# A hybrid decoder trunk on one core: delta-rule steps without GpSimd, z tiles between the k and v tiles, and a transpose in place of half of the inverse products

## Chip, cores, metric

The kernel runs on one core of a Trainium2 chip. The metric is the device time of one execution in microseconds (us), as the median of several runs. Engine names in the profile: PE is TensorE, DVE is VectorE, ACT is ScalarE, POOL is GpSimd, SP is SyncE, which issues the weight loads.

## What is computed

Two layers, each a half-step SwiGLU FFN, a token mixer and a second half-step FFN, on 336 tokens (256 prompt, 64 decode tokens of 8 sequences, 16 meta tokens), width 1024, FFN width 2816, all in float32. The mixer's input projection gives q, k, v, z (512 columns each), two gates, and b, c, h of a short convolution group. The reference, cut to what the change touches:

```python
qkv = silu(causal_dw_conv(qkv_ext, conv_gdn))
q = l2_normalize(q) * DK ** -0.5;  k = l2_normalize(k)
G = cumsum(g); diff = G[..., :, None] - G[..., None, :]
d_strict = exp(where(strict, diff, -inf)); d_incl = exp(where(incl, diff, -inf))
tmat = beta[..., None] * (k @ k.T) * d_strict + eye
u = triangular_solve(tmat, beta * v)              # and w, from k
qk = (q @ k.T) * d_incl
nv = u - w @ s;  o = (q * exp(G)) @ s + qk @ nv;  s = e_last * s + k_tail.T @ nv
o = rms_norm(o) * silu(z);  out = concat([o, gate_b * conv(gate_c * h_in)]) @ w_out
```

## The kernel before

**Products.** Each float32 product is made of three one-pass products in fp32r: a weight chunk lands in `RAW`, ACT copies its high part to `WH` (L694), DVE subtracts to get the low part `WL` (L939), and PE multiplies XH by WH, XL by WH and XH by WL (L1310 to L1312, the helper `three`). There are three chunk slots. ACT and DVE split chunk c+2 (`split_ahead`) while PE works on chunk c. Chunks are split in two halves, "hi" on ACT and "lo" on DVE.

**FFN.** 22 up chunks (gate and up tile of 128 features each), then 8 output tiles. `entry` interleaves the first two chunks as the input's tiles arrive. DVE's `up_tile(c)` scales both tiles (GR, UR: L1021, L1022), splits chunk c+2 unless c is 0, then does HF and HL (L1027, L1029). So chunk 3 is split in `up_tile(1)`.

**Mixer.** `mixer_steps` writes one list of steps that all engines walk, each doing its own share. The 28 tiles of the projection come in the order of `PROJ`: 12 of qkv (q, k, v), 4 z, 4 b, then c and h in pairs. From tile 4 on a tile is cut into three parts (`("part", i, p)`: 3, 3 and 2 of its 8 k steps), and the stretch behind each part is a slot, numbered from 0. Other work is put in slots by hand (`slot_work`): the gates (`gate_cols`, `gate_g`, `cum`, `gb`), the convolution of a qkv tile (`tap` on ACT, three taps on DVE in `conv` L1053, `silu` on ACT), the sums of squares (`sq` on ACT, `sq_rows` on PE L1496), `norms`, the scores `qk` and `kk` of each of the three token blocks t (order 2, 0, 1). A planner (`fill`) puts the delta-rule steps of `delta_stages` in the free room, at most two with PE products a slot, with LAG 2 slots between a step and what needs it.

**The triangular inverse**, per block t: `pair` (POOL, L654) masks DA into MI, `unit` (DVE, L1185) subtracts it from the identity, `nt` is its transpose (PE L1461, copied to NI by ACT L862). Then for each level m = 2, 4, ... (six levels for blocks 0 and 1, three for block 2): `x` is DA times NI, masked into XB (DVE L1191); `y` and `yt`, planned as one step, are the correction of NI and that of its transpose MI, four 128x128 products each (PE L1463), subtracted by DVE (L1196, L1200). POOL also masks QKM (L660) beside `x` of level 2.

**PSUM.** Products of four heads (L1463) and transposes (L1461) rotate over banks 5 to 7: a group waits until the one three before it has been read (`bank_free`); the third (`gb` of block 2) waits for the reading of tile 4 too, which had bank 7. A waiting instruction holds back all behind it on its engine.

## Time and profile before

| | us |
|---|---|
| median of 3 runs | 1552.85 |
| lowest, highest | 1552.75, 1554.69 |
| profiled execution: device time | 1553.45 |
| its span, first to last instruction | 1551.7 |
| PE busy | 1474.9 |
| DVE busy | 882.7 |
| ACT busy | 608.3 |
| POOL busy | 58.5 |

The span is one execution; engines overlap, so the busy times are not to be added. PE's granted clock is given per stretch: 1.00 is 2.4 GHz, 0.50 is 1.2 GHz, and a value between them is a stretch that has both. The two layers show nearly the same pattern 768 us apart; times below are of layer 0.

### The profile page before, as it was taken

Reading aid. Unit: us, or ns where it says so; the run is one execution under the profiler, and the core shown is the slowest. Engines: PE = TensorE matmul, PEld = TensorE weight load, DVE = VectorE, ACT = ScalarE, POOL = GpSimd, SP = SyncE. Lnnn points to the kernel's source line nnn. Section 1 sums busy time; section 2 is a strip of 40 time slices with the busy share of each in tenths; the row PEclk is TensorE's granted clock in tenths of the full one; section 3 lists DMA queues with packets and bytes.
Section 4 is the critical chain, followed back from the end, with each engine's and each line's share of the span. In section 5 each row is a group of like instructions: output and inputs, shape, how many; then the busy total and the mean of one; then the engine's idle time right before and its main releaser. Section 6 shows DMA issues by size and latency. Waiting matters only on the chain.

```text
span 1551.7 us, 22995 instructions
## 1 busy us (share of the span) xinstructions
PE 1474.9 (95%) x9696; PEld 1431.4 (92%) x9696; DVE 882.7 (57%) x1471; ACT 608.3 (39%) x953; POOL 58.5 (4%) x144
## 2 busy tenths in 40 slices
PE   6999999998999999999989999999899999999996
PEld 6999999878988999999989999998799889999996
DVE  4655534786458665554375554357854676656433
ACT  4533434552213543433354433345422235443431
POOL 0000001012000000000000000010210000000001
PEclk9999999999999999999999999999999999999998
DMA  7444344221113344434454443432211143444342
GB/s 262 136 136 147 123 146 156 69 94 59 37 46 129 124 137 150 148 119 149 144 187 136 137 147 128 148 121 91 88 45 56 55 144 121 138 149 155 130 150 90
DMA packets 48613, 191.11 MB, mean 123 GB/s; under 512 B 6048, under 2 KB 7328, under 8 KB 48000
## 3 DMA queue, kind: packets, MB, share of 16 engines
q1 hardware_dynamic: 47520, 183.22, 35.9%
q0 software_dynamic: 992, 6.44, 1.0%
q8 instruction: 77, 1.26, 0.3%
q14 instruction: 24, 0.20, 0.0%
HBM read 183.20 MB, written 6.43 MB: 122 GB/s over the span
## 4 chain that ended last, share of the span: by engine, by line
PE 84%; DVE 9%; ACT 4%; issue 2%; DMA 1%; SPq 1%; POOL 0%; DVEq 0%; ACTq 0%; POOLq 0%
PE PS L1310 23%; PE PS L1312 22%; PE PS L1311 22%; PE PS L1463 6%; DVE CV L1053 2%; DVE WL L939 2%; PE PS L1350 2%; PE PS L1355 2%; PE PS L1351 2%; PE PS L1618 1%; PE PS L1570 1%; DMA RAW<-in_w_up 1%; ACT WH L694 1%; PE PS L1461 1%; DVE X L997 1%
## 5 line engine op out<-in xcount | busy, mean ns | idle before, releaser
L1310 PE MATMUL PS<-XH,WH 128*128 128x336 f32 (+1 forms) x1728 | 558.3, 323 | 7.6 <-DVE WL L939 6.6
L1312 PE MATMUL PS<-XH,WL 128*128 128x336 f32 (+1 forms) x1728 | 547.1, 317 | 0.0
L1311 PE MATMUL PS<-XL,WH 128*128 128x336 f32 (+1 forms) x1728 | 546.5, 316 | 0.0
L939 DVE TENSOR_TENSOR WL<-RAW,WH 128x1024 fp32r<-128x1024 f32 (+1 forms) x312 | 399.3, 1303 | 198.3 <-ACT WH L694 198.2
L694 ACT ACTIVATE WH<-RAW 128x1024 fp32r<-128x1024 f32 (+1 forms) x312 | 345.8, 1120 | 214.7 <-DMA RAW<-in_w_down 172.5
L1310 PEld LDWEIGHTS PS<-XH,WH 128*128 128x128 f32 x1728 | 327.7, 190 | 28.2 <-issue 25.0
L1311 PEld LDWEIGHTS PS<-XL,WH 128*128 128x128 f32 x1728 | 328.2, 190 | 0.0
L1312 PEld LDWEIGHTS PS<-XH,WL 128*128 128x128 f32 x1728 | 327.8, 190 | 0.0
L1310 PE MATMUL PS<-HH,WH 128*128 128x336 f32 (+1 forms) x704 | 221.0, 314 | 0.0
L1312 PE MATMUL PS<-HH,WL 128*128 128x336 f32 (+1 forms) x704 | 220.4, 313 | 0.0
L1311 PE MATMUL PS<-HL,WH 128*128 128x336 f32 (+1 forms) x704 | 220.2, 313 | 0.0
L1021 DVE TENSOR_TENSOR GR<-PS,RB 128x336 f32<-128x336 f32 (+1 forms) x88 | 44.3, 503 | 194.8 <-PE PS L1312 194.7
L1311 PEld LDWEIGHTS PS<-HL,WH 128*128 128x128 f32 x704 | 132.4, 188 | 0.0
L1312 PEld LDWEIGHTS PS<-HH,WL 128*128 128x128 f32 x704 | 132.2, 188 | 0.0
L1310 PEld LDWEIGHTS PS<-HH,WH 128*128 128x128 f32 x704 | 132.1, 188 | 0.0
L762 ACT ACTIVATE HH<-HF 128x336 fp32r<-128x336 f32 (+1 forms) x88 | 42.4, 482 | 208.4 <-DVE HF L1027 208.4
L760 ACT ACTIVATE SG<-GR 128x336 f32<-128x336 f32 (+1 forms) x88 | 42.2, 480 | 118.1 <-DVE GR L1021 118.1
L1350 PE MATMUL PS<-XH,WH 128*128 128x336 f32 (+1 forms) x192 | 65.3, 343 | 23.3 <-DVE WL L939 12.6
L1029 DVE TENSOR_TENSOR HL<-HF,HH 128x336 fp32r<-128x336 f32 (+1 forms) x88 | 44.4, 505 | 48.2 <-ACT HH L762 48.2
L1351 PE MATMUL PS<-XH,WL 128*128 128x336 f32 (+1 forms) x192 | 64.4, 339 | 0.0
L1350 PEld LDWEIGHTS PS<-XH,WH 128*128 128x128 f32 x192 | 40.2, 209 | 24.8 <-DVE WL L939 12.5
L1053 DVE SCALAR_TENSOR_TENSOR CV<-EXT,PAR_ALL,CV 128x360 f32<-128x360 f32 x72 | 42.5, 592 | 17.7 <-ACT CV L789 16.0
(223 smaller groups left out, 1370.8 us busy)
## 6 DMA issues: line engine op xcount, KB each, us to landing
RAW<-in_w_up SPq DMA_DIRECT2D x176, 512.0 KB, 4.7
RAW<-in_w_down SPq DMA_DIRECT2D x64, 704.0 KB, 4.1
RAW<-in_w_in SPq DMA_DIRECT2D x56, 512.0 KB, 4.5
RAW<-in_w_out SPq DMA_DIRECT2D x16, 512.0 KB, 4.3
SEQ_S<-in_states SPq DMA_DIRECT2D x2, 2048.0 KB, 10.6
out_state_s<-SEQ_S POOLq DMA_DIRECT2D x2, 2048.0 KB, 8.4
X<-in_x SPq DMA_DIRECT2D x8, 168.0 KB, 6.1
out_y<-X POOLq DMA_DIRECT2D x8, 160.0 KB, 2.1
```

The source lines that it names most:

```text
L694: act.activation(WH[slot][:, cols], RAW[slot][:, cols], ACT.Copy).then_inc(split_hi.sem, 1)
L762: act.activation(hidden(HH, c, n), HF[k][:, 0:n], ACT.Copy).then_inc(h_hi.sem, 1)
L939: dve.tensor_tensor(WL[slot][:, cols], RAW[slot][:, cols], WH[slot][:, cols].bitcast(F32), ALU.subtract).then_inc(split_lo.sem, 1)
L1021: dve.tensor_tensor(GR[k][:, 0:n], PS[:, up_bank(c, 0), 0:n], RB[:, 0:n], ALU.mult).then_inc(gate_scaled.sem, 1)
L1029: dve.tensor_tensor(hidden(HL, c, n), HF[k][:, 0:n], hidden(HH, c, n).bitcast(F32), ALU.subtract).then_inc(h_lo.sem, 1)
L1053: ins = dve.scalar_tensor_tensor(cv, src[:, n, tap:tap + length - taps + 1], PAR_ALL[:, layer, col:col + 1], cv, ALU.mult, ALU.add)
L1310: pe.matmul(out, wh, xh, start=first, stop=False)
L1311: pe.matmul(out, wh, xl, start=False, stop=False)
L1312: return pe.matmul(out, wl, xh, start=False, stop=last)
L1350: pe.matmul(out, wh, XH[:, kt, 0:n], start=(kt == 0), stop=False)
L1351: pe.matmul(out, wl, XH[:, kt, 0:n], start=False, stop=False)
L1463: ins = pe.matmul(out[:, h, :], lhsT(h), rhs(h), start=True, stop=True)
```

## The change

1. **GpSimd leaves the delta steps.** `pair` goes; its product is done on DVE inside `unit`, which now follows `kk` of its block directly. QKM's mask goes: `gb` takes the minimum with a table (0 where kept, -1e4 elsewhere) instead of with 0, so the exponential is zero there.
2. **`mirror`.** `yt` stays only at the last level. At the others MI is made by four transposes of NI on PE, and ACT copies them. `y` is a step of its own; `x` of the next level waits for `y`, `y` of the next level for `mirror`.
3. **Tile order.** `TILES` puts z tiles between k and v tiles. v's convolutions move to slots 22 to 37, `silu` of z goes right behind its tile. `cum`, `gb` and the convolutions of the first tiles go a slot later, and evacuations of tiles 2 and 3 behind `gate_cols`.
4. **Table load.** ACT loads the table of Exp at the start of the mixer, ahead of the first taps.
5. **FFN.** Chunk 3 is split in `up_tile(0)`, on ACT ahead of that tile's Silu.
6. **Buffers.** XM0 and XM1 lie over SQX and ACCY; EXT's v tiles lie beyond NI and MI, so the units need wait only for POOL's copies of q and k (`qk_hist`).

```diff
-NO_PRODUCTS = ("pair", "unit", "o_inv", "o_low", "spread")
+NO_PRODUCTS = ("unit", "o_inv", "o_low", "spread", "mirror")
+TILES = [("qkv", n) for n in range(6)] + [("z", 0), ("qkv", 6), ("qkv", 7), ("z", 1), ("qkv", 8), ("z", 2), ("qkv", 9), ("z", 3),
...
-        after["pair", t] = []
-        after["unit", t] = [(("pair", t), LAG)]
+        after["unit", t] = []
         for m in levels:
-            after["x", t, m] = [(("nt", t) if m == 2 else ("yt", t, m // 2), LAG)]
-            after["yt", t, m] = [(("x", t, m), LAG)]
+            after["x", t, m] = [(("nt", t) if m == 2 else ("y", t, m // 2), LAG)]
+            if m < levels[-1]:
+                after["y", t, m] = [(("x", t, m), LAG)]
+                after["mirror", t, m] = [(("y", t, m), LAG)]
...
-    slot_work[2] += [("cum",), ("lo", 1, 1)]
-    slot_work[3] += [("gb", ORDER[0]), ("gb", ORDER[1])]
+    slot_work[2] += [("lo", 1, 1)]
+    slot_work[3] += [("cum",)]
+    slot_work[4] += [("gb", ORDER[0])]
+    slot_work[5] += [("gb", ORDER[1]), ("gb", ORDER[2])]
...
+    earliest.update({("unit", t): scores_at + 2 * n + 2 for n, t in enumerate(ORDER)})
...
                 for c in range(N_UP):
-                    if c > 0:
+                    if c == 0:
+                        split_ahead(layer, AT_UP[s] + 1)
+                    elif c > 1:
                         split_ahead(layer, AT_UP[s] + c)
                     up_tile(c, c % 2)
...
             def mixer(layer):
+                act.preload_act_table(ACT.Exp)
...
+                    elif what == "mirror":
+                        evacuated(act.activation(MI[:, step[1], :, :], group(step, layer), ACT.Copy))
...
-                    if c > 0:
-                        split_ahead(layer, AT_UP[s] + c)
+                    if c != 1:
+                        split_ahead(layer, AT_UP[s] + max(c, 1))
...
-                            ins = dve.tensor_scalar(DA[:, t, h, :], gb[:, h, :], GC[:, t, h:h + 1], 0.0, ALU.subtract, ALU.min)
+                            ins = dve.scalar_tensor_tensor(DA[:, t, h, :], gb[:, h, :], GC[:, t, h:h + 1], barred(t),
+                                                           ALU.subtract, ALU.min)
...
-                        dve.wait_ge(pair_part.sem, pair_part.at(NTH["pair", t], layer))
+                        own(("kk", t), layer)
+                        ch.step(dve.tensor_tensor(MI[:, t, :, :], DA[:, t, :, :], heads_of(mask("pair")), ALU.mult))
...
+                    elif what == "mirror":
+
+                        evacuated(("y", *step[1:]), layer)
+                        t = step[1]
+                        per_head_products(step, layer, lambda h: NI[:, t, h, :], None, transpose=True)
```

**DVE from the scores to the units.** Before: from `norms`' last instructions on; L1171 and L1174 are `qk`, L1053 a convolution, L1179 `kk`, L1070 to L1073 the reading of a qkv tile, L1185 the units.

```order
L1171 TENSOR_TENSOR QKV<-QKV,QKM 128x4x128
L1174 TENSOR_TENSOR QKM<-PS,DA 128x512
L1053 SCALAR_TENSOR_TENSOR CV_118<-EXT,PAR_ALL,CV_118 128x360 x3
L1179 SCALAR_TENSOR_TENSOR DA<-PS,TOK,DA 128x128 x4
L1171 TENSOR_TENSOR QKV<-QKV,QKM 128x4x128
L1174 TENSOR_TENSOR QKM<-PS,DA 128x512
L939 TENSOR_TENSOR WL_55<-RAW_52,WH_58 128x1024
L1086 TENSOR_TENSOR ZS<-PS,RB 128x336
L1179 SCALAR_TENSOR_TENSOR DA<-PS,TOK,DA 128x128 x4
L939 TENSOR_TENSOR WL_55<-RAW_52,WH_58 128x1024
L1185 TENSOR_TENSOR MI<-MK,MI 128x512 x3
```

Of the change, the same place from the first `qk` on (L1187 and L1190 are `qk`, L1101 the reading of a z tile, L1195 `kk`, L1203 and L1204 `unit`, L954 a split):

```order
L1187 TENSOR_TENSOR QKV<-QKV,QKM 128x4x128
L1190 TENSOR_TENSOR QKM<-PS,DA 128x512
L1101 TENSOR_TENSOR ZS<-PS,RB 128x336
L1195 SCALAR_TENSOR_TENSOR DA<-PS,TOK,DA 128x128 x4
L1203 TENSOR_TENSOR MI<-DA,MK 128x512
L1204 TENSOR_TENSOR MI<-MK,MI 128x512
L1187 TENSOR_TENSOR QKV<-QKV,QKM 128x4x128
L1190 TENSOR_TENSOR QKM<-PS,DA 128x512
L1195 SCALAR_TENSOR_TENSOR DA<-PS,TOK,DA 128x128 x4
L954 TENSOR_TENSOR WL_55<-RAW_52,WH_58 128x1024
```

The first unit stands behind one `qk` and one `kk`, where all three stood behind three of each, and each unit has two instructions.

**ACT from the gates to the first convolution.** Before (L843 and L845 are `gate_cols`, L849 to L852 `cum`; L858 and L860, three times, `gb`; L807 the first Silu, L789 its neighbour `tap`):

```order
L845 ACT_TABLE_LOAD
L845 ACTIVATE TOK<-TOK 128x12
L694 ACTIVATE WH_60<-RAW_54 128x1024 x2
L849 ACT_TABLE_LOAD
...
L860 ACTIVATE QKM<-PS 128x512
L807 ACT_TABLE_LOAD
L807 ACTIVATE QKV<-CV_117 128x256
L808 ACTIVATE QKV<-CV_117 128x16
L809 ACTIVATE QKV<-CV_117 128x64
L789 ACTIVATE CV_117<-EXT,PAR_ALL 128x360
```

Of the change (L858 is `gate_cols`' Ln, L862 `cum`, L873 `gb`, L704 a split, L819 the Silu, L801 the tap):

```order
L858 ACT_TABLE_LOAD
L858 ACTIVATE TOK<-TOK 128x12
L704 ACTIVATE WH_60<-RAW_54 128x1024 x2
L862 ACT_TABLE_LOAD
...
L873 ACTIVATE QKM<-PS 128x512
L704 ACTIVATE WH_58<-RAW_52 128x1024
L819 ACT_TABLE_LOAD
L819 ACTIVATE QKV<-CV_117 128x256
L820 ACTIVATE QKV<-CV_117 128x16
L821 ACTIVATE QKV<-CV_117 128x64
L801 ACTIVATE CV_117<-EXT,PAR_ALL 128x360
```

A weight split now stands ahead of the first Silu and its table load.

**DVE at the head of an FFN**, before (L1021 and L1022 are GR and UR, L1027 and L1029 HF and HL of `up_tile`):

```order
L1021 TENSOR_TENSOR GR_108<-PS,RB 128x336
L1022 TENSOR_TENSOR UR_110<-PS,RB 128x336
L1027 TENSOR_TENSOR HF_114<-SG_112,UR_110 128x336
L1029 TENSOR_TENSOR HL<-HF_114,HH 128x336
L1021 TENSOR_TENSOR GR_109<-PS,RB 128x336
L1022 TENSOR_TENSOR UR_111<-PS,RB 128x336
L939 TENSOR_TENSOR WL_55<-RAW_52,WH_58 128x1024 x2
```

and of the change:

```order
L1036 TENSOR_TENSOR GR_108<-PS,RB 128x336
L1037 TENSOR_TENSOR UR_110<-PS,RB 128x336
L954 TENSOR_TENSOR WL_55<-RAW_52,WH_58 128x1024 x2
L1042 TENSOR_TENSOR HF_114<-SG_112,UR_110 128x336
L1044 TENSOR_TENSOR HL<-HF_114,HH 128x336
```

The two halves of chunk 3 are split four instructions earlier.

## Rows read from the trace of the kernel before

**Rows 1.** The page, part 1: busy us (share of the span) and instructions.
```profile
PE 1474.9 (95%) x9696; PEld 1431.4 (92%) x9696; DVE 882.7 (57%) x1471; ACT 608.3 (39%) x953; POOL 58.5 (4%) x144
```
**Rows 2.** Waits of PE, whole span: us in total, times, longest.
```profile
PE PS L1461 <- DVE MI L1185: 11.1, 4, 5.0
...
PE PS L1310 <- DVE WL L939: 7.9, 6, 1.7
PE PS L1522 <- DVE SEQ_GB L1144: 5.5, 2, 2.8
```
**Rows 3.** Windows of 10 us: busy of each engine, granted clock (PEclk), DMA share, GB/s.
```profile
355.00:365.00 10.00, 5.45 (x24) 5.00 (x25) 7.70 (x10) 1.33 (x3) 8.02 (x5) 0.66 0.31 103
...
405.00:415.00 10.00, 10.00 (x83) 9.99 (x83) 3.17 (x7) 4.56 (x11) 0.00 (x0) 1.00 0.23 87
```
**Rows 4.** Timeline of the gates: start us, us, instruction [idle before <-releaser].
```profile
293.59 1.28 ACT L845 ACT_TABLE_LOAD   x1
...
296.07 0.59 PE L1522 MATMUL PS<-TOK,MK 128*128 128x4 f32 x2 [2.76 <-DVE SEQ_GB L1144]
...
298.97 0.17 DVE L1070 TENSOR_TENSOR EXT<-PS,RB 128x16 f32<-128x16 f32 x1
```
**Rows 5.** Timeline, from the first Silu to the third `sq_rows`.
```profile
308.43 1.28 ACT L807 ACT_TABLE_LOAD   x1
...
311.14 2.36 DVE L1053 SCALAR_TENSOR_TENSOR CV<-EXT,PAR_ALL,CV 128x360 f32<-128x360 f32 x4 [3.34 <-ACT CV L789]
...
319.77 1.09 PE L1496 MATMUL PS<-SQX,MK 128*8 128x336 f32 x2 [1.88 <-ACT SQX L840]
```
**Rows 6.** Timeline, from `norms` to the first transposes.
```profile
341.48 0.50 DVE L1151 TENSOR_TENSOR RB<-RB 128x336 f32<-128x336 f32 x1
...
357.18 5.10 DVE L1185 TENSOR_TENSOR MI<-MK,MI 128x512 f32<-128x512 f32 x3
...
358.99 1.11 PE L1461 MATMUL PS<-MK,MI 128*128 128x128 f32 x4 [5.01 <-DVE MI L1185]
...
361.43 0.63 PE L1310 MATMUL PS<-XH,WH 128*128 128x336 f32 x1
```
**Rows 7.** Timeline of PE in two places of the inverse.
```profile
384.21 1.05 PE L1463 MATMUL PS<-XM,MI 128*128 128x128 f32 x8
385.10 1.06 PE L1463 MATMUL PS<-MI,XM 128*128 128x128 f32 x8
...
440.50 0.32 PE L1310 MATMUL PS<-XH,WH 128*128 128x336 f32 x1
440.97 0.60 PE L1461 MATMUL PS<-MK,QKV 128*128 128x128 f32 x4
441.40 1.06 PE L1463 MATMUL PS<-NI,DA 128*128 128x128 f32 x8
```
**Rows 8.** Groups by form: busy us, mean ns of one, idle before.
```profile
L1191 DVE TENSOR_TENSOR XM<-PS,MK 128x512 f32<-128x512 f32 x24 | 16.6, 690 | 33.3 <-PE PS L1463 33.3
...
L1179 DVE SCALAR_TENSOR_TENSOR DA<-PS,TOK,DA 128x128 f32<-128x128 f32 x24 | 6.7, 341 | 0.0
...
L862 ACT ACTIVATE NI<-PS 128x512 f32<-128x512 f32 x6 | 3.6, 598 | 24.2 <-PE PS L1461 24.2
```
**Rows 9.** The page, part 6: a weight load; KB each, us from issue to landing.
```profile
RAW<-in_w_up SPq DMA_DIRECT2D x176, 512.0 KB, 4.7
```
**Rows 10.** Timeline at the head of the first FFN.
```profile
29.66 11.26 SPq L584 DMA_DIRECT2D RAW<-in_w_up  x5
...
36.98 0.51 DVE L1021 TENSOR_TENSOR GR<-PS,RB 128x336 f32<-128x336 f32 x1
...
38.98 1.99 ACT L694 ACTIVATE WH<-RAW 128x1024 fp32r<-128x1024 f32 x2
...
40.36 2.35 DVE L939 TENSOR_TENSOR WL<-RAW,WH 128x1024 fp32r<-128x1024 f32 x2
...
41.72 0.39 PE L1310 MATMUL PS<-XH,WH 128*128 128x336 f32 x1 [1.63 <-DVE WL L939]
```

More of the change, by code:

```diff
@@ L41 @@
 EPS = 1e-6
+BARRED = -1e4
 G_HIST, S_HIST = GW - 1, SW - 1
@@ L509, in decoder_trunk @@
         STEPS = mixer_steps()
-        MASKED = [step[1] for step in STEPS if step[0] == "x" and step[2] == 2]
         SEQ_G = SEQ_GB[:, :, :]
@@ L554, in tokens, with silu_of @@
             return T if f < 2 * DEPTH - 1 else N_PROMPT + N_SAMPLE
+        def silu_of(kind, n, layer):
+            return act_out.at(SILUS.index((kind, n)), layer)
         def hidden(buf, c, n):
@@ L799, in silu @@
             def silu(layer, i):
-                kind, n = PROJ[i]
+                kind, n = TILES[i]
                 if kind == "z":
@@ L1550, in mixer @@
                         t = step[1]
+                        if step[2] > 2:
+                            evacuated(("mirror", t, step[2] // 2), layer)
                         per_head_products(step, layer, lambda h: MI[:, t, h, :], lambda h: XB[t][:, h, :])
@@ L1555, in mixer @@
                         t = step[1]
+                        evacuated(("mirror", t, step[2] // 2), layer)
                         per_head_products(step, layer, lambda h: XB[t][:, h, :], lambda h: MI[:, t, h, :])
@@ L1684, in constants @@
     found["lv8_meta"] = found["lv8"] & (row >= META_AT)
+    for name in ("full", "seq"):
+        found[f"bar_{name}"] = np.where(found[f"incl_{name}"], 0.0, BARRED)
     masks = np.stack([np.broadcast_to(found[name], (P, P)) for name in MASKS], axis=1).astype(np.float32)
```

132 lines of the change are left out of this document (66 added, 66 removed).

## The prediction

> **What bounds the kernel now.** I read the page's busy shares first, then the waits of PE, then the timeline around each long wait. PE is busy for 95% of the span [rows 1], so what can be won is PE's own work, the time it waits, and what it runs at half clock after a wait. The waits name three places with one engine in front: the first transposes of the inverse wait 11.1 us for DVE's units, the head of the FFNs 7.9 us for a low part, the gates' sums 5.5 us for SEQ_GB [rows 2]. The reader should see in the windows that the first costs more than its wait: around it the granted clock is 0.66, where a window farther on, with PE full, has 1.00 [rows 3]. 0.66 over 10 us is 6.8 us at the lower level.
>
> **The unit, per layer.** DVE starts `norms` at 341.48 and its three units begin only at 357.18, since all three `kk`, a convolution or two and two splits stand ahead; PE waits 5.01 us, restarts at 358.99 and begins the next part at 361.43 after two groups of transposes with, by the waits, 5.6 us of waiting per layer (11.1 us over two layers) [rows 2, 6]. The three subtractions take 5.10 us, 1.7 each, beside POOL's products, where an instruction of that size takes 0.69 without them [rows 6, 8]. After the change the first unit stands behind `norms` (1.5, an estimate from its six small instructions), one `qk` (two of 0.69), the reading of a z tile (0.5, an estimate by half again the 336-column kind), one `kk` (four of 0.34 that overlap, 1.1) and its own two instructions (1.4): 5.9 us where it was 17.5 (341.48 to 358.99) [rows 6, 8]. PE in the same stretch has three parts (3 matmuls go in 0.47, so a part of three k steps takes 1.4 and one of two 0.9) and three groups of four-head products at 0.89 (384.21 to 385.10) [rows 7]. From `qk` of block 2 to `nt` of block 2 that is 7.9 us of PE from the slot's start. A convolution (three taps of 0.6 [rows 5], 1.8) stands ahead of `norms`, so DVE needs 1.8 + 5.9 = 7.7 plus what it lags, some 0.7. I count waits of 0.5 for the first transposes. After that DVE has the harder load: until unit 0 another 5.8 us (`qk` 1.4, `kk` 1.1, split 1.2, tile 0.7, unit 1.4), against some 4.6 us of PE: wait 1.0. Unit 1 comes 5.9 us later (`qk` 1.4, split 1.2, `kk` 1.1, mask 0.7, unit 1.4), which PE covers but for 0.3. So new waits of 1.9 us stand against 5.6. The half clock goes too: from 358.99 it lasted until about 364.4 (0.66 is 6.8 us, begun during the wait), 5.4 us of which 0.6 waiting, so half of 4.8 = 2.4 us of PE time comes back. Sum: 5.6 + 2.4 - 1.9 = **6.1 per layer**. Bounds: 3 (DVE is 3 us later than walked, and each unit waits 1 us longer) and 8.0 (no wait is left).
>
> **`mirror`, per layer.** Twelve of fifteen `yt` groups go (five each for blocks 0 and 1, two for block 2) and twelve groups of four transposes come. A group of products takes 0.89, one of transposes 0.43 (440.97 to 441.40) [rows 7]. PE has nothing to wait for in this stretch (busy 10.00 of 10 [rows 3]), so the difference counts in full: 12 x 0.46 = **5.5 per layer**. DVE loses twelve subtractions; ACT gets twelve copies of 0.60 [rows 8], hidden, since ACT is busy 4.56 of 10 us there [rows 3]. If that cover went, each would cost at most what the copy takes. As new waits I put 0.8 per layer: near slot 37 a convolution and a split on DVE stand ahead of an `x`, whose bank the third group behind it wants. Bounds 0 and 4.
>
> One rule speaks against the transposes. The window at 405 to 415 holds three groups of transposes and stays at 1.00 [rows 3]; by that the clock is not touched. The Trainium skill (TensorE: Matmul & The Clock Gate, Part 4: PE-mode transpose) says that a transpose does not count as busy for the clock gate. By it, more transposes would invite more stretches at the lower level; I keep it as a rival.
>
> **Gates and convolutions, per layer.** This is the part that I trust least. PE waited 2.76 us for SEQ_GB and ran at half clock behind it; then 1.88 us at the third `sq_rows` [rows 4, 5]. Now `cum` stands one part later (1.4 us of cover) and `gate_g` starts 0.5 us earlier: evacuations of tiles 2 and 3, 1.1 together (an estimate), move behind `gate_cols`, and the Exp load of 1.28 us [rows 4] is gone from the chain, but the first convolution still stands ahead of `gate_g`. Left: a wait of 1.2. The next is new: `gb` of block 2 needs bank 7, so the reading of tile 4, which DVE does at 298.97 [rows 4] behind a split and a convolution, as before; PE is there at 298.0: wait 1.2. A third: `gb` of block 1 waits for `cum` to be read by ACT, a table load (1.28) and four small ones behind DVE's `cum`, which now stands behind a split: 0.7. Then ACT splits half a chunk (1.0 [rows 10]) before the Silu load, so that the first Silu starts at about 308.5, 1.2 us sooner than now (308.43 + 1.28 = 309.71 [rows 5]). DVE waits for that tap as before (3.34 us [rows 5]), and a split now stands ahead of the convolution of tile 4, so the third `sq_rows` is reached by its input at about 319.4: no sooner than now (319.77 [rows 5]), but with one more part of 1.4 us done. Gain at full clock: 0.4 + 1.4 = 1.8 us, with PE waits of 1.2 + 1.2 + 0.7 + 1.4 + 2.9 = 7.4 us before it. I cannot tell whether the clock falls: 1.63 us of waiting left it alone at the FFN (the first matmul behind it takes 0.39 us), 1.88 us lowered it (a matmul of 1.09) [rows 5, 10]. If it falls at the gates, the chain there lengthens by up to 2.6 us; behind the third `sq_rows` it costs 1.3. I take **0.5 per layer**, bounds -2 and 5 (both old waits gone with their half clock).
>
> What hides the added work: `unit`'s product and the q, k, v readings lie on DVE beside PE, which is the longer of the two from slot 30 on. The minimum with a table costs what the scalar one did, 0.34 [rows 8]. The masks of QKM are removed from POOL, on no path.
>
> **FFN, twice per layer.** PE waits 1.63 us for chunk 3's low part, which DVE begins at 40.36, behind HF, HL, GR and UR [rows 10]. Now it begins behind the first UR, at 36.98 + 0.9 = 37.9; its raw half was issued at 29.66 and lands 4.7 us later [rows 9, 10], the high part (1.0 a half) is done by 36.8, so the low half is there at 39.1, before PE wants it at 41.72 - 1.63 = 40.1. HF and HL of chunk 0 come 2.4 us later; PE needs their bank only for chunk 3, which waits for UR alone, and h itself at the down products. What is late next is chunk 4: wanted at 46.8, its low half there at about 46.4. So 2 x 1.63 = **3.3 per layer**; bounds 2.6 and 3.3.
>
> **Sum.** 6.1 + 5.5 - 0.8 + 0.5 + 3.3 = 14.6 per layer, 29.2 for two. The profiled execution took 1553.45 us, 1.75 more than its span and 0.6 above the median of the runs, so the median becomes 1552.85 - 29.2 = **1524 us**. The bounds together: 2 x (8.0 + 5.5 + 5 + 3.3) = 44 gives 1509; 2 x (3 + 5.5 - 4 - 2 + 2.6) = 10 gives 1543.
>
> **Rivals.**
> - *ACT and DVE keep pace*, and the waits at the gates and at `sq_rows` go with their half clock: 5 instead of 0.5 per layer, 9 us more: 1515. For it speaks that z tiles bring DVE 0.5 us where a q tile brings 0.6 and 1.8 of convolution; against it that the chain over two table loads and the first tap is as long as before [rows 5].
> - *DVE stays the bound at the units.* It lags, and transposes wait as long as now. Then only `mirror`, FFN and the gates count: 5.5 - 0.8 + 0.5 + 3.3 = 8.5 per layer: 1536. DVE is full there before the change, and gets three more instructions of 0.69 per layer; against it, a convolution and POOL's slowing of 3 us leave the stretch.
> - *Transposes lower the clock.* If in each layer four stretches of 3.4 us (half of the 6.8 above) ran at half speed, each would cost 1.7: 14 us more, 1538. Only the skill's rule speaks for it; transposes in a window at 1.00 speak against it [rows 3].
> - *Slower: the copies of `mirror` come late.* A `mirror` queued on ACT behind a split (1.0) and a scaled four-head copy holds up `y` of the next level and the group three behind. It decides from 29.2 / 24 = 1.2 us of PE waiting per `mirror`; at 1.5 us the time is 1560. Against it: two slots lie between them, at least two parts and some groups, 4 us of PE.
>
> **Chances.** Forecast 0.60; pace kept 0.12; DVE the bound 0.18; transposes 0.05; slower 0.04; no change to speak of 0.01. The range 1511 to 1538 leaves out the edge of the first rival and the last three in part. A change under 0.2% (3 us) can't be told from none. Faster 0.95, same 0.01, slower 0.04.
>
> **What would show it.** In the profile after: no transposes waiting 5 us for MI, but `nt` waits of 0.3 to 1.0; the FFN waits of 1.6 for L954 gone; 24 groups of eight records of XM and MI fewer, 96 transposes of NI in their place, at full clock; around 290 to 320 several PE waits of 1 to 3 us, for SEQ_GB, for the reading of tile 4, for SQX. The prediction is wrong if those last are gone or have become longer than 7.4 us together, if DVE reaches the first unit more than 3 us behind PE, or if `mirror`'s copies appear among what PE waits for.

## The result and the profile after

The changed kernel, called *after* below, takes **1517.5 us** (median of 4 runs, 1514.5 to 1521.6) where the kernel before took 1552.8 on the same chip (4 runs, 1552.5 to 1554.7): a ratio of 0.9772, 95% interval 0.9747 to 0.9797, so 35.4 us less, within 4. The profiled execution is the slowest of the four, 1521.55 us with a span of 1519.7, 32.0 shorter than that of before. The others have spans down to 1512.7 at a mean granted clock of 0.988, where this one has 0.978.

The page, part 1, and the waits of PE over the whole span (us in total, times, longest) answer to [rows 1] and [rows 2]:

```profile
PE 1458.1 (96%) x9600; PEld 1418.2 (93%) x9600; DVE 868.0 (57%) x1453; ACT 618.8 (41%) x977; POOL 41.9 (3%) x132
...
PE PS L1329 <- DVE WL L954: 6.5, 4, 1.8
...
PE PS L1329 <- issue: 2.9, 2, 1.4
PE PS L1515 <- ACT SQX L853: 2.8, 2, 1.4
PE PS L1480 <- DVE MI L1204: 2.2, 2, 1.1
...
PE PS L1541 <- DVE SEQ_GB L1159: 1.7, 2, 0.8
```

PE has 96 instructions fewer and its wait for the units fell from 11.1 us to 2.2, that for SEQ_GB from 5.5 to 1.7. The row for WL deceives: 7.9 us became 6.5, but none of the old four waits at the heads of the FFNs is in it. Its four waits stand in the mixers, two per layer: one is new, and the other, at the mixer's end, is 1.75 us where it was 0.65.

**Where the time went.** Each stage has one group of matmuls at its start and one at its end, so a stage can be measured between two rows. Here are those of the first mixer after the change; in every kernel below I read the same two.

```profile
L1354 PE MATMUL PS<-MK,ACCX x6: 166/250/250, 287.8 to 288.3; 128*128 128x1 f32 x6
```
```profile
L1456 PE MATMUL PS<-MK,SQY x6: 250/250/271, 514.6 to 515.2; 128*128 128x1 f32 x6
```

| stage, us | before | after | |
|---|---|---|---|
| FFN, three of the four (the last is 10 shorter) | 229.7 | 227.7 | -2.0 each, -7.9 for four |
| mixer, first and second layer | 241.5, 241.3 | 226.8, 226.5 | -14.7, -14.8 |
| start, up to the first FFN | 33.3 | 36.2 | +2.9 |
| the five passages between stages, and the tail | | | +2.5 together |

The last two rows are not the change's. The start lies between 33.0 and 33.8 us in all thirteen other profiles, with and without the edits. Here the granted clock from 13 to 36 us is 0.93, where it was 1.00 before. The passages contain short stretches of half clock whose length varies from run to run.

A mixer can be cut further, at the last of the eight `sq_rows` and at the part of the projection behind which slot 30 begins. The first row here is of before, whose part begins at 361.43 [rows 6]; the other two are of after.

```profile
334.36 0.73 PE L1496 MATMUL PS<-SQX,MK 128*8 128x336 f32 x2
```
```profile
335.24 0.73 PE L1515 MATMUL PS<-SQX,MK 128*8 128x336 f32 x2
...
357.33 0.40 PE L1329 MATMUL PS<-XH,WH 128*128 128x336 f32 x1
```

| stretch of the mixer, us (first, second layer) | before | after |
|---|---|---|
| start to the last `sq_rows` | 48.1, 48.0 | 47.4, 47.4 |
| to slot 30 (the units) | 27.1, 27.1 | 22.1, 22.1 |
| to the mixer's end (the inverse and what follows) | 166.3, 166.2 | 157.3, 157.0 |

Inside the first mixer, the timeline of PE and DVE from `norms` to the transposes answers to [rows 6]:

```profile
339.31 0.50 DVE L1166 TENSOR_TENSOR RB<-RB 128x336 f32<-128x336 f32 x1
...
343.78 0.69 DVE L1203 TENSOR_TENSOR MI<-DA,MK 128x512 f32<-128x512 f32 x1
344.51 0.69 DVE L1204 TENSOR_TENSOR MI<-MK,MI 128x512 f32<-128x512 f32 x1
...
345.60 0.60 PE L1480 MATMUL PS<-MK,MI 128*128 128x128 f32 x4
...
351.39 0.66 PE L1480 MATMUL PS<-MK,MI 128*128 128x128 f32 x4 [1.10 <-DVE MI L1204]
```

The first unit is ready 5.9 us after `norms` begins (339.31 to 345.2), and the first transposes wait for nothing; those of block 0 wait 1.10. A window of 10 us over the units, and one over the levels of the inverse, answer to [rows 3]:

```profile
345.00:355.00 10.00, 8.89 (x68) 8.57 (x68) 9.22 (x21) 2.63 (x4) 0.73 (x2) 1.00 0.00 1
...
400.00:410.00 10.00, 10.00 (x80) 9.90 (x80) 5.85 (x11) 5.83 (x13) 0.00 (x0) 1.00 0.01 3
```

The clock there is 1.00 where it was 0.66. Ahead of it, the timeline of PE at the gates and convolutions answers to [rows 4, 5]:

```profile
297.08 0.39 PE L1541 MATMUL PS<-TOK,MK 128*128 128x4 f32 x2 [0.83 <-DVE SEQ_GB L1159]
...
313.80 0.73 PE L1515 MATMUL PS<-SQX,MK 128*8 128x336 f32 x2 [1.42 <-ACT SQX L853]
316.04 0.62 PE L1329 MATMUL PS<-XH,WH 128*128 128x336 f32 x1 [1.51 <-DVE WL L954]
...
322.64 0.73 PE L1515 MATMUL PS<-SQX,MK 128*8 128x336 f32 x2
```

The wait of 1.51 at 316.04 was not foreseen: PE wants the low half of chunk 4, and DVE makes it behind the convolution of tile 3, though it had sat idle for 4.83 us before tile 2's. The third `sq_rows`, at which the record puts 2.9 us, waits for nothing, since PE comes late: the first matmul behind the 1.51 takes 0.62, half clock.

### The profile page after: what moved, and what is told of

Read it like the earlier page. It is cut to its first block, busy times and chain, and to the rows that moved or that the text cites. A ratio compares the mean times of both kernels' runs of the same rounds, so it can differ in the third digit from the quotient of the medians.

```text
span 1519.7 us, 22795 instructions
## 1 busy us (share of the span) xinstructions
PE 1458.1 (96%) x9600; PEld 1418.2 (93%) x9600; DVE 868.0 (57%) x1453; ACT 618.8 (41%) x977; POOL 41.9 (3%) x132
## 4 chain that ended last, share of the span: by engine, by line
PE 90%; DVE 5%; ACT 2%; issue 1%; DMA 1%; SPq 1%; POOL 0%; DVEq 0%; ACTq 0%; POOLq 0%
PE PS L1329 25%; PE PS L1331 24%; PE PS L1330 24%; PE PS L1482 5%; PE PS L1369 2%; PE PS L1374 2%; PE PS L1370 2%; PE PS L1480 1%; DVE CV L1068 1%; DVE WL L954 1%; PE PS L1645 1%; DMA RAW<-in_w_up 1%; PE PS L1515 1%; PE PS L1597 1%; ACT WH L704 0%
## 5 line engine op out<-in xcount | busy, mean ns | idle before, releaser
L954 DVE TENSOR_TENSOR WL<-RAW,WH 128x1024 fp32r<-128x1024 f32 (+1 forms) x312 | 398.4, 1300 | 200.9 <-ACT WH L704 200.9
L704 ACT ACTIVATE WH<-RAW 128x1024 fp32r<-128x1024 f32 (+1 forms) x312 | 343.9, 1118 | 207.8 <-DMA RAW<-in_w_down 171.6
L1329 PEld LDWEIGHTS PS<-XH,WH 128*128 128x128 f32 x1728 | 326.8, 189 | 23.9 <-issue 20.8
```

Of the source, the lines that this page charges most:

```text
L704: act.activation(WH[slot][:, cols], RAW[slot][:, cols], ACT.Copy).then_inc(split_hi.sem, 1)
L954: dve.tensor_tensor(WL[slot][:, cols], RAW[slot][:, cols], WH[slot][:, cols].bitcast(F32), ALU.subtract).then_inc(split_lo.sem, 1)
L1329: pe.matmul(out, wh, xh, start=first, stop=False)
```

## The experiments

All ratios are against the kernel before on the same chip. A difference "by the ratios" is that of two ratios times 1552.8; after's own interval is wide, so such a difference from after is uncertain by about 4.4 us, one between two experiments by about 3. Where less is at stake I go by the stages of the profiles.

### The FFN edit alone

```diff
-                    if c > 0:
-                        split_ahead(layer, AT_UP[s] + c)
+                    if c != 1:
+                        split_ahead(layer, AT_UP[s] + max(c, 1))
```
(and the same on ACT, put into the kernel before)

> The kernel before with the FFN edit alone: DVE and ACT split chunk 3 behind the first two products of chunk 0, not behind HF and HL. Everything of the mixer is as before. Theory (each 1.63 us wait of PE at the head of an FFN is worth its length and a little half clock behind it, 2.0 us as the stages of the two profiles say): four times 2.0 = 8.0 us less, 1544.9; by the record's 1.63 it would be 6.5, 1546.3. The mixer stage (PE's first matmul on the mixer's columns to the first of the out-projection) stays at 241.4 us in both layers. Rival (part of what the FFN stages gained comes out of the mixer's changes, since the split of chunk 3 competes with other work there): the FFN stages shorten by less than 1 us each and the kernel is at 1549 or above.

Measured: 1546.8, ratio 0.9951 (0.9938 to 0.9963), so 7.6 us less. The FFN stages are 227.8, 227.8, 227.7 and 217.9, each 1.9 to 2.0 shorter, and the mixers 241.2 and 241.1. The theory holds: the edit is worth the same alone and in company.

It is worth more than the 1.63 us of the wait. PE's matmuls before the change show why:

```profile
39.62 0.32 PE L1311 MATMUL PS<-XL,WH 128*128 128x336 f32 x1
39.77 0.32 PE L1312 MATMUL PS<-XH,WL 128*128 128x336 f32 x1
...
41.95 0.32 PE L1311 MATMUL PS<-XL,WH 128*128 128x336 f32 x1
42.10 0.33 PE L1312 MATMUL PS<-XH,WL 128*128 128x336 f32 x1
```

Matmuls start every 0.155 us but last 0.32. The idle time is counted from the end of the last, 0.16 after the next would have started. The L1312 of 42.10 comes 2.33 behind that of 39.77 where 0.46 is the rule: 1.87 us lost for a wait of 1.63. So some 0.25 is to be added to this wait; for others of PE I take the same as an estimate.

### Mirror by products

```diff
-                        per_head_products(step, layer, lambda h: NI[:, t, h, :], None, transpose=True)
+                        per_head_products(step, layer, lambda h: NI[:, t, h, :], lambda h: mask("ident"))
```

> The kernel after, with the 12 mirror groups of each layer made by products (N times the identity mask) in place of transposes: the same values by another form of matmul, all else as after. Theory of the record (a group of four-head products takes 0.46 us more of PE than one of transposes, nothing covers it, and transposes do not touch the clock): 24 x 0.46 = 11.0 us more than after, 1528.5, with the mixer stage 5.5 us longer in each layer. Rival 1 (the exchange of products for transposes was hidden, and what the mixer gained came from the waits alone): not over 1 us more in a layer, 1517 to 1519.5. Rival 2 (transposes invite half clock): more products raise the granted clock in the inverse, which gives back part, so the kernel is under 1524.

Measured: 1531.1, ratio 0.9851 (0.9838 to 0.9865): 12.3 us more than after by the ratios, 0.51 a group; the mixers take 232.5 and 234.0, 5.7 and 7.5 more. PE's timeline of this kernel has the price itself, the group of four products standing where in after (second fence) four transposes stand:

```profile
368.86 1.06 PE L1482 MATMUL PS<-MK,NI 128*128 128x128 f32 x8
369.75 1.06 PE L1482 MATMUL PS<-NI,DA 128*128 128x128 f32 x8
```
```profile
372.85 0.60 PE L1480 MATMUL PS<-MK,NI 128*128 128x128 f32 x4
373.28 1.06 PE L1482 MATMUL PS<-NI,DA 128*128 128x128 f32 x8
```

From start to start 0.89 against 0.43, the 0.46 on record. The window from 400 to 410 is at 1.00 with the products, as in after with the transposes, so neither rival stands: the exchange is not hidden and gives nothing back through the clock. On the contrary, this kernel has one spell of half clock of 3.4 us behind slot 30 in each layer (383.0 to 386.4 in the first) that after has not; what such spells cost is worked out under "Old tiles and no mirror".

### Without mirror, and mirror alone

```diff
-            if m < levels[-1]:
-                after["y", t, m] = [(("x", t, m), LAG)]
-                after["mirror", t, m] = [(("y", t, m), LAG)]
-            else:
-                after["yt", t, m] = [(("x", t, m), LAG)]
+            after["yt", t, m] = [(("x", t, m), LAG)]
```

> The kernel after without mirror: the transposed inverse is again kept by twelve more groups of products per layer, with DVE's subtraction, each beside its y group, as in the kernel before; all else as after. By the price per group that the mirror made by products has just shown (12.3 us for 24 groups, by the ratios 0.9851 and 0.9772, 0.51 each), and with DVE loaded by twelve subtractions more per layer but no copies on ACT: Theory A (the whole worth of mirror is PE's price for a group, DVE's load does not count): 11 to 13 us more than after, 1529 to 1531. Theory B (DVE's twelve subtractions of 0.69, 8.3 us per layer, count as well, since DVE is behind in this stretch): 3 or more us per layer on top, 1535 or above. Theory C (the longer chain y, mirror, y costs waits that the old form does not have, 0.8 per layer on record): 1527 to 1528.5.

Measured: 1530.6, ratio 0.9848 (0.9834 to 0.9861), 11.8 more than after by the ratios; mixers 232.0 and 233.4. Theory A: this kernel and the last, which differ by twelve subtractions per layer on DVE and twelve copies on ACT, are alike, so DVE's relief is worth nothing that shows, and PE's products are the whole.

The opposite, mirror put into the kernel before:

> The kernel before with mirror alone: twelve groups of products per layer become transposes, copied by ACT; the units, tiles, gates and FFN are as before. Theory (PE is full in the levels of the inverse in the kernel before too, so mirror is worth there what it is worth in after): 10 to 13 us less than before, 1541 to 1544. Rival 1 (in before the levels start behind a late unit, the queue of groups is denser, and the chain y, mirror, y, one link longer than y, x, y, makes waits): 5 to 9 us less, 1545 to 1549. Rival 2 (transposes bring half clock into the inverse's levels): mean clock of the profile under 0.97 and 1549 or more.

Measured: 1543.9 (one run of four at 1537.4), ratio 0.9925 (0.9903 to 0.9947), 11.6 less than before; mixers 237.9 and 234.3, 3.6 and 7.0 less. The inverse's levels are at full clock with transposes there as well, by the window over them:

```profile
367.00:447.00 80.00, 79.48 (x627) 78.00 (x626) 37.32 (x70) 27.76 (x56) 0.32 (x2) 1.00 0.16 53
```

PE is busy in 79.48 of 80. The first theory holds and both rivals fall.

### The unit's product back on POOL

```diff
+                    elif what == "unit":
+                        pool.wait_ge(evac["dve"].sem, evac["dve"].at(LEFT_PSUM["kk", t][1], layer))
+                        ...
+                        pool.tensor_tensor(MI[:, t, :, :], DA[:, t, :, :], heads_of(mask("pair")),
+                                           ALU.mult).then_inc(pair_part.sem, 1)
...
-                        ch.step(dve.tensor_tensor(MI[:, t, :, :], DA[:, t, :, :], heads_of(mask("pair")), ALU.mult))
+                        dve.wait_ge(pair_part.sem, pair_part.at(NTH["unit", t], layer))
```

> The kernel after, with the unit's first product (DA times the pair mask) back on POOL behind each kk, and DVE waiting for it before its subtraction; the masks in QKM stay on ACT's exponential and the order of steps is that of after. Theory A (the gain at the units came from taking POOL out of the chain, which before needed 2.4 us of POOL and stretched DVE's subtraction from 0.69 to 1.7 us): DVE has 0.69 less of its own and waits for POOL instead; the first transposes wait 2 to 4 us per layer more than after, with half clock behind them: 5 to 12 us more, 1522 to 1530. Theory B (it came from the order alone: each unit right behind its own kk, with two steps between): POOL's product is done before DVE gets there or costs under 1 us per layer: 1515.5 to 1519.5.

Measured: 1522.2, ratio 0.9794 (0.9781 to 0.9808); 3.4 more than after by the ratios, which alone would be too little to tell; the mixers take 229.4 and 228.6, 2.6 and 2.1 more, and the stretch from the last `sq_rows` to slot 30 takes 24.9 and 23.9 where after has 22.1. That is less than Theory A and more than B. POOL's and DVE's timelines of the first two units, and the wait of PE:

```profile
340.51 1.27 POOL L676 TENSOR_TENSOR MI<-DA,MK 128x512 f32<-128x512 f32 x1 [5.44 <-DVE DA L1201]
```
```profile
341.82 0.69 DVE L1207 TENSOR_TENSOR MI<-MK,MI 128x512 f32<-128x512 f32 x1 [1.39 <-POOL MI L676]
...
348.68 0.69 DVE L1207 TENSOR_TENSOR MI<-MK,MI 128x512 f32<-128x512 f32 x1 [1.65 <-POOL MI L676]
```
```profile
349.42 0.84 PE L1483 MATMUL PS<-MK,MI 128*128 128x128 f32 x4 [2.09 <-DVE MI L1207]
```

DVE waits 1.39 and 1.65 for a product that it would make itself in 0.69, and PE waits 2.09 for unit 0 where it waited 1.10, at half clock behind. POOL takes 1.27 here. In the kernel before the groups by form give it 2.03, and DVE's subtraction beside it 1.7 instead of 0.69 [rows 6]:

```profile
L654 POOL TENSOR_TENSOR MI<-DA,MK 128x512 f32<-128x512 f32 x6 | 12.1, 2027 | 5.8 <-DVE DA L1179 5.8
```

Here, where DVE mostly waits while POOL works, neither is slowed. I infer that most of what POOL cost before was that six products and three subtractions were bunched at one place, and that freeing the order ended that by itself; no run shows it alone, since none has the new order of tiles with the units bunched as before.

### The old order of tiles

```diff
-TILES = [("qkv", n) for n in range(6)] + [("z", 0), ("qkv", 6), ("qkv", 7), ("z", 1), ("qkv", 8), ("z", 2), ("qkv", 9), ("z", 3),
-                                         ("qkv", 10), ("qkv", 11)] + [("b", n) for n in range(4)]
+TILES = [("qkv", n) for n in range(12)] + [("z", n) for n in range(4)] + [("b", n) for n in range(4)]
```

> The kernel after, with the projection's tiles in the order of before (z 0 to 3 behind v 3), all other edits kept. Theory A (z tiles give DVE stretches without a convolution just where it lags, so it reaches the first unit soon; without them the convolutions of v stand denser ahead of norms, qk and kk): three convolutions of 1.8 us and readings move ahead of the first unit against PE's 4.2 us per z tile, PE waits 2 to 4 us for the first transposes per layer: 4 to 12 us more, 1521 to 1529. Theory B (the tiles' order only changes which tile fills PE while DVE is not late anyway): within 2 us of after, 1515.5 to 1519.5.

The slots of v's convolutions are worked out from the places of their tiles, so this edit moves them too, from 22, 28, 34 and 37 back to 18, 20, 23 and 25, and the transposes of v may come earlier.

Measured: 1534.2, ratio 0.9868 (0.9855 to 0.9881): 14.9 more than after, mixers 232.7 and 235.6. It is the dearest edit by the median, not clear of mirror's 11.8 to 12.3, and more than Theory A gave. The loss lies at the units: from the last `sq_rows` to slot 30 it takes 28.6 and 31.3 us where after has 22.1, and from there to the end no longer than after (156.9 and 156.1). The timeline has a wait of 2.31 for the first unit, which in after has none, and one of 2.43 for that of block 0. PE's view first, then why DVE is late:

```profile
345.92 0.87 PE L1479 MATMUL PS<-MK,MI 128*128 128x128 f32 x4 [2.31 <-DVE MI L1203]
354.70 0.66 PE L1479 MATMUL PS<-MK,MI 128*128 128x128 f32 x4 [2.43 <-DVE MI L1203]
```
```profile
341.46 1.84 DVE L1067 SCALAR_TENSOR_TENSOR CV<-EXT,PAR_ALL,CV 128x360 f32<-128x360 f32 x3
...
346.50 0.69 DVE L1189 TENSOR_TENSOR QKM<-PS,DA 128x512 f32<-128x512 f32 x1
348.88 1.85 DVE L1067 SCALAR_TENSOR_TENSOR CV<-EXT,PAR_ALL,CV 128x360 f32<-128x360 f32 x3 [1.69 <-ACT CV L800]
350.65 1.12 DVE L1194 SCALAR_TENSOR_TENSOR DA<-PS,TOK,DA 128x128 f32<-128x128 f32 x4
```

A convolution of 1.84 stands between `qk` and `kk` of block 2, ahead of the first unit, and another between those of block 0, where it costs its own 1.85 and 1.69 of waiting for ACT's tap. The order with z tiles moves them, wait and all, out of this place.

### Old tiles and no mirror

This joins the last edit and that of "Without mirror".

> The kernel after with both the old order of tiles and no mirror: of the change there stay the unit on DVE behind its kk, the masks in the exponential, the gates one slot later and the FFN edit. Each edit taken out alone cost 14.9 (tiles) and 11.8 us (mirror), by the ratios. Theory A (they are separate stretches, the first ends where the inverse's levels begin): the two add, 1517.5 + 26.7 = 1544, so units, gates and FFN alone are worth 10 us against before, of which the FFN 7.6. Theory B (with old tiles DVE is late and PE waits anyway, so that PE's extra products fall into waits): they overlap by 4 us or more, 1540 or less.

Measured: 1540.5, ratio 0.9915 (0.9898 to 0.9931), 22.2 above after, where the parts add to 26.7; mixers 237.0 and 237.4. The median has Theory B's overlap, 4.5, but with an interval of over 4, and I found no wait in which the products hide: PE is busy in all of 365 to 445. The stretch behind slot 30 says where the overlap comes from, and it is the clock:

| from slot 30 to the mixer's end, first and second layer | us | of them at half clock |
|---|---|---|
| after | 157.3, 157.0 | none |
| mirror by products | 164.4, 164.4 | 3.4, 3.4 |
| without mirror | 163.8, 163.8 | 3.4, 3.4 |
| old tiles | 156.9, 156.1 | 3.4, none |
| old tiles and no mirror | 161.6, 161.6 | none |
| before | 166.3, 166.2 | 6.4, 6.2 |
| mirror alone | 162.7, 159.2 | 10.4, 2.9 |

```profile
352.00:515.80 163.80, 158.91 (x1126) 150.16 (x1123) 98.11 (x206) 49.27 (x96) 4.19 (x16) 0.99 0.24 87
```
```profile
360.50:522.10 161.60, 157.19 (x1126) 148.47 (x1124) 93.31 (x193) 48.24 (x87) 2.88 (x11) 1.00 0.25 87
```

The first window is of the kernel without mirror, the second of this one. What half clock costs is in the rows of before:

```profile
362.13 0.48 PE L1312 MATMUL PS<-XH,WL 128*128 128x336 f32 x1
362.41 0.48 PE L1310 MATMUL PS<-XH,WH 128*128 128x336 f32 x1
```

Matmuls start every 0.28 us there and every 0.155 at full clock, so that 3.4 us of half clock cost 1.5. With that taken off, mirror is worth 5.0 to 6.1 us per layer in all four comparisons (after with each of the two below it, old tiles with and without mirror, before with and without it), as 12 x 0.46 = 5.5 says. The two edits then add, as Theory A has it: three spells, 4.5 us together, lie in the kernels that lack one of the edits and none in this one. Each profile is one execution, so the medians need not have the same spells. Against before, what is left of the change is worth 13.2 us by the ratio, of which the FFN 7.6.

### The gates one slot earlier, and no early table load

```diff
-    slot_work[2] += [("lo", 1, 1)]
-    slot_work[3] += [("cum",)]
-    slot_work[4] += [("gb", ORDER[0])]
-    slot_work[5] += [("gb", ORDER[1]), ("gb", ORDER[2])]
+    slot_work[2] += [("cum",), ("lo", 1, 1)]
+    slot_work[3] += [("gb", ORDER[0]), ("gb", ORDER[1])]
+    slot_work[4] += [("gb", ORDER[2])]
```

> The kernel after, with the gates' sums one slot earlier again (cum in slot 2, the three gb in slots 3, 3 and 4). Theory (the shift by a part gives DVE and ACT 1.4 us more before PE asks for SEQ_GB and for the first gb): PE waits some 2.2 us for SEQ_GB instead of 0.83 and 1.2 for the reading of tile 4, half clock follows as before the change, and ACT's exponentials start as early as DVE's cum: 1.4 to 3 us more per layer, 1520.5 to 1523.5. Rival (PE's waits there are swallowed, since the chain over two table loads and the first tap sets when sq_rows can go, and PE reaches them with a wait anyway): within 1 us of after, 1516.5 to 1518.5.

Measured: 1518.6, ratio 0.9768 (0.9755 to 0.9782). PE waits 2.2 us per layer for SEQ_GB instead of 0.83, as the theory says, and the time does not show it: the rival's outcome. The mixers take 229.1 and 225.8, 2.3 more and 0.7 less than in after, which is no clearer.

```diff
             def mixer(layer):
-                act.preload_act_table(ACT.Exp)
```

> The kernel after without the early load of Exp's table at the mixer's start. Theory (it takes a table load of 1.28 us out of the chain to gate_g, so to SEQ_GB and cum): PE waits up to 1.3 us more for SEQ_GB than 0.83, with half clock behind it, and the first Silu comes later too: 1 to 2.5 us more per layer, 1519.5 to 1522.5. Rival (ACT stood idle there, and the load is made behind gate_cols before DVE needs it; a second load at 301.96 stays in both): within 1 us of after, 1516.5 to 1518.5.

Measured: 1517.9, ratio 0.9772 (0.9755 to 0.9788). SEQ_GB is waited for 1.4 us instead of 0.83. The median is the rival's, but the profiled execution, the slowest of the four at 1523.0, does not bear it out: its mixers take 228.3 and 230.3, and the last `sq_rows` is reached 1.3 and 0.9 us later than in after. A cost of 1 us per layer is not ruled out.

### The low half of chunk 4 early

```diff
+    slot_work[7].remove(("lo", 2, 0))
+    slot_work[6].insert(1, ("lo", 2, 0))
+    slot_work[7].remove(("hi", 2, 1))
+    slot_work[7].insert(1, ("hi", 2, 1))
```

> The kernel after, with two steps moved in slots 6 and 7: DVE makes the low half of chunk 4 before the third convolution (while it sits 4.83 us idle for ACT's tap, 306.31 to 311.14), and ACT squares tile 0 before it splits the second half of chunk 4. Theory (PE's waits of 1.42 for SQX at 313.80 and 1.51 for WL at 316.04, with the half clock behind them, are real costs): both go or fall under 0.5, the window 315 to 325 is back at a granted clock near 1.00, and 2 to 5 us go per layer, 1508 to 1514, unless the third sq_rows, which in after waits for nothing because PE comes late, now waits: then 0.5 to 2 per layer, 1513.5 to 1516.5. Rival (what these waits cost is given back at the third sq_rows in full, the chain of taps and convolutions sets the time): within 1 us of after.

Measured: 1516.7, ratio 0.9764 (0.9751 to 0.9778), 1.2 under after and not to be told from it; mixers 225.6 and 225.6, 1.2 and 0.9 shorter. The waits of 1.42 and 1.51 are gone (0.32 is left of the first), the window from 306 to 325 is at 1.00, and the third `sq_rows` now waits:

```profile
309.27 0.73 PE L1519 MATMUL PS<-SQX,MK 128*8 128x336 f32 x2 [0.32 <-ACT SQX L857]
...
315.66 0.73 PE L1519 MATMUL PS<-SQX,MK 128*8 128x336 f32 x2 [1.83 <-ACT SQX L857]
```

So the expectation's second branch came. Yet the chain gives back only a part: the last `sq_rows` is reached 44.6 and 44.7 us from the mixer's start, where after has 47.4, of which 1.5 is the clock, as the last section shows. Behind slot 30 this execution then loses 1.4 to 1.6 again (158.7 and 158.6 us), with one spell of half clock of 3.4 us in each layer that after has not. The first begins at 379.2, just behind a wait of 0.45 which after has too, without such a spell.

### The mixer's end

The other pair of waits for weights lies at the end of after's mixer: 1.45 us at 481.41 ("issue" in the page) and 1.75 behind it, for WL. First three moves on top of the last kernel:

```diff
+    steps.remove(("o_low", 1))
+    steps.remove(("lo", 12, 0))
+    at = steps.index(("hi", 12, 0))
+    steps[at:at + 1] = [("o_low", 1), ("hi", 12, 0), ("lo", 12, 0)]
```
(and the low part of the mixed rows ahead of chunk 15's second low half)

> The kernel after with the two moved steps of e7 and three more at the mixer's end: DVE takes the last o_low while it sits 2.13 us idle for ACT's tap (475.55 to 477.68 in after), then the low half of chunk 14, ahead of the last-but-one convolution, and makes the low part of the mixed rows ahead of the second low half of chunk 15. In after PE waits 1.45 at 481.41 and 1.8 us for WL there, 3.2 per layer. Theory: both go, but the low part of the mixed rows (needed 0.5 us before it is there in after) comes only some 2.3 us sooner, so 1.5 to 2.5 us per layer are won beside what e7 wins: 1511.5 to 1514. Rival (the wait moves in full to the low part of the mixed rows): within 1 us of e7, 1515.5 to 1517.5.

Measured: 1517.3, ratio 0.9762 (0.9747 to 0.9776): the rival's outcome, but not by its wait. The 1.45 is gone and PE waits 2.12 for the low half of chunk 15, with a clock of 0.93 from 475 to 500:

```profile
481.96 0.42 PE L1339 MATMUL PS<-OH,WH 128*128 128x336 f32 x1 [2.12 <-DVE WL L962]
```

So that half, too, went ahead of the last convolution (and on ACT its high half ahead of the last tap), and one more group of PE's ahead of the mixed rows:

```diff
-    steps += tail + [("out_o", 0), ("out_o", 1), ("out_o", 2), ("out", 0), ("out", 1), ("out_o", 3)]
+    steps += tail + [("out_o", m) for m in range(4)] + [("out", 0), ("out", 1)]
...
-                        convolve(layer, 2 * N_IN - 1)
                         nxt = ahead(layer, AT_OUT - 1, 2)
                         split_low(*nxt, 0)
+                        convolve(layer, 2 * N_IN - 1)
+                        split_low(*nxt, 1)
```

> The kernel of e9 with the mixer's end mended further, after its profile: there the wait of 1.45 was gone, but PE waited 2.12 us at 481.96 for the low half of chunk 15, which DVE makes at 480.68 behind the last convolution, with half clock behind it (0.93 from 475 to 500). Now ACT makes the first high half of chunk 15 while it is idle for the last tile (474.4 to 478.26), DVE its low half ahead of the last convolution, the second low half comes in DVE's wait for the high part of the mixed rows, and PE does the fourth half of the out-projection's rows ahead of those that want the mixed rows' low part. Theory: by the times in e9 the low half is there at 479.4 where PE wants it at 479.84, the mixed rows' low part at 484.1 where PE now wants it at 483.9: the wait goes but for 0.5, 1.6 us and 1 to 2 us of half clock per layer are won, 1511 to 1514. Rival (the chain evacuation, tap, convolution, high part, low part of the last tile sets the end, and any wait ahead of it only moves there): within 1 us of e9, 1516 to 1518.

Measured: **1510.5** (1509.6 to 1513.4), ratio 0.9728 (0.9714 to 0.9741), the fastest here: 5.3 us under the last kernel and 6.8 under after by the ratios, just below the theory's 1511 to 1514. The mixers take 222.6 and 222.4; from slot 30 to the end they take 155.6 and 155.5, where the last kernel has 158.6 and 158.5. The only wait left there is 0.67, and the window is at full clock:

```profile
482.00 0.42 PE L1341 MATMUL PS<-OH,WH 128*128 128x336 f32 x1 [0.67 <-DVE WL L964]
```
```profile
475.00:500.00 25.00, 24.32 (x156) 23.77 (x155) 15.91 (x27) 11.65 (x21) 3.22 (x5) 1.00 0.58 223
```

The rival that any wait only moves falls. Of the 3.0 us per layer, 1.45 is the shorter wait and some 1.5 the half clock that is gone. The three moves (DVE's, ACT's and PE's) were made together, so what each is worth is not known.

## Why the prediction was right, and where it was off

It said 1524 with 1511 to 1538; 1517.5 came, 6.5 us faster. Every term has the right sign, and all are somewhat small. The time is nearer to the rival at 1515 than to the forecast, but not by that rival's mechanism: it had 5 us per layer at the gates, and 1.6 came. Per layer, from the stages and the timeline:

| term | on record | measured |
|---|---|---|
| unit, up to slot 30 | 6.1 | 7.8 |
| mirror, less its waits, to the mixer's end | 4.7 | 5.3 |
| gates and convolutions | 0.5 | 1.6 |
| FFN, two | 3.3 | 3.9 to 4.0 |
| sum | 14.6 | 18.7 |

Twice 18.7 is 37.4; the start and the passages of this execution take 5.4 back, which leaves the 32.0 of the spans. The ratio's 35.4 lies between.

- **Unit.** The walk was right where it could be checked: 5.9 us from `norms` to the first unit on record, 5.9 measured. The term was mis-sized. From the last `sq_rows` to slot 30 took 27.1 us and takes 22.1; in it 0.9 us less of parts and three groups, 2.2 us, more are done, and 1.5 of half clock behind it went: 5.0 - 0.9 + 2.2 + 1.5 = 7.8. Of new waits 1.9 was on record (its own 0.5, 1.0 and 0.3 make 1.8); 0, 1.10 and 0 came. Left out was a wait of 0.34 of before, at the `qk` of block 1 (347.33), that went as well, and what a wait costs beyond its row. The attribution needs mending: the record names the early unit and POOL's slowing as the gain, with the z tile as one reading of 0.5 in the walk. The runs show that with the old tiles units, masks and gates without POOL are worth 5.6 us in all (13.2 less 7.6), and that the tiles' order, with the slots of v's convolutions, adds 10 to 15. Whether the tiles alone would do it, with the units bunched behind three `kk`, no run tries. The rival "DVE stays the bound at the units", 1536, is close to what the old tiles give: 1534.
- **`mirror`.** The price of 0.46 is shown by direct exchange, and the whole of it counts. The 0.8 of new waits for its copies did not come: they appear among no waits. To the 5.5 comes a spell of half clock of before that after lacks (3.4 us long at 456 to 460, so 1.5), and from it go 1.7 for longer waits: those at the mixer's end, for the low halves of weights above all, are 3.7 in place of 1.1, and those ahead of them 0.9 less. That makes 5.3, which is measured. The waits at the end were not foreseen, and the last two kernels are their repair.
- **Transposes and the clock.** The stretch behind slot 30 is at 1.00 in after, with 96 transposes in two layers, and at 0.99 with products in their place. The Trainium skill (TensorE: Matmul & The Clock Gate, Part 4: PE-mode transpose) says that a transpose does not count as busy for the clock gate; among the products of this stretch it did no measurable harm, and the rival of 0.05 falls. Short spells of half clock come in this stretch in kernels of either form.
- **Gates.** The step that was wrong is the walk of the waits. On record 1.2 (SEQ_GB), 1.2 (tile 4), 0.7, 1.4 (first `sq_rows`) and 2.9 (third). The profile of after has 0.83, 0, 0, 1.42 and 0, and 1.51 for a split that the walk left out, 3.8 together where 7.4 stood. The other waits are there when PE comes at full clock: the kernel without mirror, whose order is the same up to this point, waits 0.83, 0.68 for the reading of tile 4, 0.25 for `cum`'s evacuation, 1.27, 1.51 and 0.46 at the third `sq_rows`, 5.0 in all, and 0.28 and 0.37 at two later ones. Each was put too high or, at the first `sq_rows`, right; the 2.9 most of all. The last `sq_rows` is reached 0.7 us sooner with one more part done, one of two k steps, 0.9: 1.6. (At the third the part that is added is one of three k steps, the 1.4 on record; there after is 1.3 us later than before, 34.8 against 33.5 from the mixer's start, so that 0.1 is won where 1.8 at full clock stood.) The run with the gates a slot earlier says that their place is worth nothing that can be told; the rival "ACT and DVE keep pace" was half right.
- **FFN.** Mechanism and place as on record. The wait's 1.63 was taken for its cost, which is 1.87 by the starts; 3.3 should have been 3.8.

Taking out mirror costs 7.3 beside the old tiles and 11.8 beside the new, by the ratios; in the profiles the spells of half clock account for it. What stays open is what decides whether a spell comes.

## What to carry to other kernels

When engines share one static order, an instruction that waits for another engine should not stand between two links of a third engine's chain: the dearest edit here moved tiles, and with them convolutions and their taps, away from `qk`, `kk` and `unit`. Look for the idle time ahead of such an instruction and put there what someone else will soon want; and go on until the last wait at that place is gone, since the first repair may only uncover the next. Where PE is full, a group of transposes for one of products is worth its difference in full, and the wait of PE that was measured here cost a quarter of a microsecond more than its row says. Before two kernels are compared by a microsecond or two, count their half clock, since 3.4 us of it cost 1.5.
